# A decoder trunk on one core: identity transposes on TensorE while the program opens, and another order of the last four row tiles

## What is computed

```python
def _rms_norm(x, g):
    y = x * lax.rsqrt(jnp.mean(x * x, axis=-1, keepdims=True) + EPS)
    return y * g

def _short_conv(x, w_in, w_conv, w_out):
    b_gate, c_gate, h = jnp.split(x @ w_in, 3, axis=-1)
    u = causal_depthwise_conv(c_gate * h, w_conv)      # width 3
    return (b_gate * u) @ w_out

for layer in range(2):
    xn = _rms_norm(x, g[0])
    mix = _short_conv(xn, ...) if layer == 0 else _dilated_attention(xn, ...)
    x = x + _rms_norm(mix, g[1])
    ff = _swiglu(_rms_norm(x, g[2]), w_in, w_out)
    x = x + _rms_norm(ff, g[3])
```

## Time and profile before

| | us |
|---|---|
| median of 3 runs | 2272.85 (2272.17 to 2273.74) |
| the profiled execution, its time | 2273.41 |
| the profiled execution, its span from the first to the last instruction | 2271.6 |
| PE busy | 2216.3 (98%) |
| DVE busy | 1687.8 (74%) |
| ACT busy | 962.3 (42%) |
| POOL busy | 485.1 (21%) |
| mean granted clock of PE, share of full speed | 0.997 |

### The profile page before, as it was taken

The page is one execution under the profiler, slowest core; times in us unless marked ns, Lnnn a source line. Parts: engine busy times, 40 slices in busy tenths (PEclk is TensorE's granted clock), DMA queues, the critical chain, the costliest instruction groups (busy, mean ns, idle before and its releaser), DMA issues. The chain is left out here.

```text
span 2271.6 us, 31865 instructions
## 1 busy us (share of the span) xinstructions
PE 2216.3 (98%) x10604; PEld 1848.8 (81%) x10604; DVE 1687.8 (74%) x2529; ACT 962.3 (42%) x1758; POOL 485.1 (21%) x416
## 2 busy tenths in 40 slices
PE   7999998999999999999999999999899999999997
PEld 6888887888888888877888888888788888888886
DVE  6988769777777667797767666676877777776768
ACT  4322345322222243564566566565532222223453
POOL 5000026333333100251110011002533333310113
PEclk9999999999999999999999999999999999999999
DMA  5122242333333477635333233234133333338764
GB/s 158 38 56 56 96 155 61 102 108 98 111 98 112 157 265 241 204 122 161 84 85 84 67 73 83 57 107 144 50 113 107 102 104 105 103 108 281 246 227 171
DMA packets 246010, 278.24 MB, mean 122 GB/s; under 512 B 18528, under 2 KB 157792, under 8 KB 243808
## 3 DMA queue, kind: packets, MB, share of 16 engines
q1 hardware_dynamic: 242656, 264.84, 38.0%
q10 hardware_dynamic: 3200, 11.54, 1.5%
HBM read 202.40 MB, written 48.76 MB: 111 GB/s over the span
## 5 line engine op out<-in xcount | busy, mean ns | idle before, releaser
L1249 PE MATMUL banks<-xb_mid,up_split 128*128 128x512 f32 x2064 | 477.4, 390 | 1.5 <-DVE up_split L2381 1.5
L1249 PEld LDWEIGHTS banks<-xb_mid,up_split 128*128 128x128 f32 x2064 | 388.2, 188 | 82.5 <-DVE up_split L2381 1.9
L1338 PE MATMUL banks<-down_split 128*128 128x512 f32 x1848 | 423.0, 390 | 4.7 <-DVE down_split L2749 3.3
L1338 PEld LDWEIGHTS banks<-down_split 128*128 128x128 f32 x1848 | 345.4, 188 | 80.9 <-DVE down_split L2749 8.1
L1249 PE MATMUL banks<-xb_low,up_split 128*128 128x512 f32 x1584 | 368.8, 391 | 5.6 <-DVE xb_low L2309 2.0
L1249 PEld LDWEIGHTS banks<-xb_low,up_split 128*128 128x128 f32 x1584 | 298.1, 188 | 69.0 <-DVE up_split L2381 4.8
L2749 DVE TENSOR_TENSOR down_split<-down_raw,down_split 128x1024 fp32r<-128x1024 f32 x154 | 198.2, 1287 | 107.3 <-ACT down_split L1955 106.9
L1955 ACT CAST down_split<-down_raw 128x1024 fp32r<-128x1024 f32 x154 | 161.8, 1051 | 204.2 <-PE banks L1338 169.5
L3391 POOL TENSOR_TENSOR sums<-raw_up 128x512 f32<-128x512 f32 x88 | 117.3, 1336 | 482.3 <-DMA raw_up<-in_ffn_in_w 255.1
L1383 PE MATMUL banks<-x_hi,w_second 128*128 128x512 f32 x672 | 176.3, 394 | 0.0
L3062 DVE CUSTOM_DVE_ANT_0 scores<-banks,bias 128x896 f32<-128x896 f32 (+7 forms) x128 | 96.7, 756 | 78.8 <-PE banks L1420 63.5
(11 more groups left out here) (227 smaller groups left out, 3607.8 us busy)
## 6 DMA issues: line engine op xcount, KB each, us to landing
raw_up<-in_ffn_in_w SPq DMA_DIRECT2D x88, 512.0 KB, 5.0
down_raw<-in_ffn_out_w SPq DMA_DIRECT2D x154, 256.0 KB, 3.4
down_raw<-hid_spill SPq DMA_DIRECT2D x154, 256.0 KB, 4.1
hid_spill<-hid_mix SPq DMA_DIRECT2D x110, 256.0 KB, 4.9
down_second<-in_ffn_out_w SPq DMA_DIRECT2D x66, 256.0 KB, 3.3
k_stack<-k_parts SPq DMA_DIRECT2D x32, 512.0 KB, 6.2
hid_spill<-hid SPq DMA_DIRECT2D x44, 256.0 KB, 2.0
raw_up<-in_conv_in_w SPq DMA_DIRECT2D x18, 512.0 KB, 5.2
```

The lines of the kernel that those rows point to most:

```text
L1249: mm = pe.matmul(bank(b_out), up_part(ph, p, a)[:, q * P:(q + 1) * P], block(RIGHT_OF[p], b)[:, q, :], start=(i == 0), stop=(i == len(pass ...
L1338: mm = pe.matmul(bank(b_out), side[:, a, 0, i * P:(i + 1) * P], side[:, b, 1, :], start=(p in (M3, M5, M1, M2) and first and j == 0), stop ...
```

## The change

Three edits, all in the opening. (1) PE issues 78 transposes of the identity matrix into bank 7, whose result nobody reads: 30 before the turn of tile 0, and 16, 10, 16 and 6 behind the turns of tiles 0, 1, 2 and 3. (2) The turns of tiles 4 to 7 stand behind matmuls 1, 11, 23 and 33 of the opening instead of 8, 18, 28 and 38. (3) ACT squares tile 7 directly behind tile 6, ahead of the high part of tile 4.

```diff
-        TURNS_FIRST = {8: HT, 18: HT + 1, 28: HT + 2, 38: HT + 3}
+        TURNS_FIRST = {1: HT, 11: HT + 1, 23: HT + 2, 33: HT + 3}
+        KEPT_BUSY = (30, 16, 10, 16, 6)
...
+            def keep_busy(n):
+
+                for _ in range(n):
+                    pe.transpose(psum[:, 7, 0:P], ident[:], ident[:])
+
             pe.wait_ge(*setup_step.at("norm0", 3))
+            keep_busy(KEPT_BUSY[0])
             for t in range(TT // 2):
                 turn("norm0", t)
+                keep_busy(KEPT_BUSY[t + 1])
...
-                    if i < TT:
+                    if i < TT - 1:
                         second_square("norm0", i)
+                    if i == TT - 2:
+                        second_square("norm0", TT - 1)
                     if i >= lag_split:
                         high_part("norm0", i - lag_split)
```

## The result

The changed kernel is slower: 2276.95 us, median of 19 runs (2275.15 to 2278.9), against 2273.74 for the kernel before, of which 19 runs were now taken too (2271.22 to 2276.25). The ratio is 1.0015, 95% interval 1.0008 to 1.0022. The profiled execution has a span of 2275.1 us, 3.5 more than that of before. The prediction was 2270.5.

The account below looks back on a forecast made before the run. PE, busy 98% of the span, was taken as the bound. Terms 1.65 + 0.29 + 0.41 + 0.39 - 0.09 - 0.36 = 2.29 us off the profiled 2273.41, and 0.56 for the median, gave 2270.5; range 2268.6 to 2274.2.

Parts of the forecast that it names:

- Transposes and the clock: Opening, PE: unbroken identity transposes raise the clock from half to full at 6.8 us; up to 10.7 costs nothing.
- What full clock is worth: Opening: first eight matmuls 1.65 us, turn of tile 4 0.29, ACT's wait 0.41; together 2.35 us saved.
- The fillers are hidden by the loads of x and by ACT, and cost nothing: Opening, ahead of turn 3: 72 of the 78 fillers delay nothing if turn 3 starts by 17.2 us; price nothing.
- What the opening gives up early, the following stage passes on: Behind the opening PE waits for nothing for 230 us, so the opening's gain is handed on.
- Turns of tiles 4 to 7, square of tile 7: Opening: new waits of 0.09 and 0.36 us ahead of turns 4 and 6, 0.39 won at second half; square free.
- fall ahead of the matmuls: Rival, chance 0.25: PE idles after turn 3 and its clock falls again, price 1.55 us, 2272.1; among the turns, 2274.1.
- The rival on which the kernel becomes slower: Ahead of turn 3: identity transposes do not raise the clock, +6.9 us, 2279.7; chance 0.12.
- does not reach the end: Rival, chance 0.08: the 2.3 us won at 34 us are lost later to a load or VectorE, 2272.9.

Follow-up runs that it names:

- e4: The kernel before with 82 filler transposes (30, 16, 10, 16, 10), old places of the turns and old order of the squares; 2281.57 us, ratio 1.0036.
- e5: The changed kernel with 100 semaphore increments that nobody waits for in PE's first feed-forward layer, in front of the loop; 2270.31 us, ratio 0.9985.
- e9: The kernel before with 160 semaphore increments in PE's first feed-forward layer, no fillers, old order; 2285.78 us, ratio 1.0056.
- e10: The changed kernel with 100 semaphore increments in PE's second feed-forward layer, behind the loop; 2276.89 us, ratio 1.0019.
- e8: The changed kernel with 46 fillers (24, 8, 4, 6, 4) instead of 78; 2270.35 us, ratio 0.9985.
- e1: The changed kernel with four more fillers, ten instead of six behind the turn of tile 3; 2283.18 us, ratio 1.0045.

## Why the prediction was wrong

- *Transposes and the clock.* Right. The 30 fillers took 5.88 us, between 30 x 0.108 and 30 x 0.221; with those two prices some 22 ran slowly (an estimate), so the clock went up near 7.7 us (forecast 6.8, needed by 10.7). What full clock is worth was right too: in e4 the first eight matmuls last from 19.31 to 21.24, 1.62 us less than before (forecast 1.65). The rule of the Trainium skill ("TensorE: Matmul & The Clock Gate", Part 4: PE-mode transpose) that full clock does not engage for transposes does not hold here: nothing but transposes ran until 19.43, and the turn at 8.58 took 1.04 us.
- *The fillers are hidden by the loads of x and by ACT, and cost nothing.* This is the step that failed: right for the opening, wrong for the program. I priced a filler by its time on PE alone. Its other price is its room in PE's instruction stream: 156 instructions in front of a loop moved the loop among the packets of q8, and that cost 3.25 and 3.07 us at its two returns, shown by e5, e9 and e10.
- *What the opening gives up early, the following stage passes on.* Right as far as it went: 2.33 us earlier at 38 us, 3.11 ahead of the first stall. My view of the waits ended at 268 us, and a stall on "issue" has no releaser, so nothing in the trace of before pointed at the loop except the missing line of q8 between 1177 and 1420 us, which I did not look for.
- *Turns of tiles 4 to 7, square of tile 7.* Right in sum, wrong in the two waits. The turn of tile 4 starts at 19.88 (forecast 19.70), 0.45 us behind the first matmul; at 0.237 for a matmul that is 0.22 of waiting, where 0.09 was forecast. The turn of tile 5 starts at 23.11 (22.86). The seven matmuls ahead of the turn of tile 6 take 1.67 us (25.14 to 26.81), and 7 x 0.237 is 1.66: at most 0.1 of waiting, where 0.36 was forecast. The start of turn 6 was right all the same (26.81, forecast 26.85), since DVE's norm of tile 6 sets it (it ends at 26.76, forecast 26.81): what PE had lost ahead of turn 4 came off this wait. In all, the new order gives nothing: with it the matmuls that started at 40.30 start 0.03 us later than without it (37.97 against 37.94 in e4), where 0.06 later was forecast.
- *Rivals.* The clock did not fall ahead of the matmuls, in spite of 1.40 us of idling. The rival on which the kernel becomes slower had the wrong mechanism, and "does not reach the end" named loads of data or VectorE and a time of 2272.9, not instructions and a net loss. The range left a loss of this kind out.

That the opening's gain is real is shown by e5 and e8: 3.1 and 3.0 us under the kernel before, taken together with them (2273.39), interval 0.6 to 2.4 thousandths. A difference under the 0.2% of the prediction could therefore be told.

What is shown is that the loop's position decides and that packets are loaded inside it when it stalls; that the reason is one packet too many (A2) is an inference. What stays open: how many packets are held (seven at least, as 1602 instructions cannot lie in fewer), and whether one of them is always the next to be loaded. The shifts 0, 3, 80, 92, 126 and 256 did not stall and 156, 160 and 164 did; the first edge lies between 126 and 156, the second between 164 and 256, and neither was tried closer. If A2 holds, 1602 instructions touch eight packets from 65 of the 256 starting places, so the second edge would lie 65 behind the first, between 191 and 221; this is an estimate that no run tested.

## What to carry to other kernels

Count the instructions that a change puts in front of a loop as well as their time, and compare the packets on the engine's instruction queue inside the loop before and after: if they go from none to some, the returns may stall on "issue" as here, and no semaphore shows for it. If a useful edit stalls a loop, move the loop, by padding to the next whole packet (e5) or by making the edit smaller (e8), before giving up the edit.

## What the runs showed of the hardware

Whether a loop of 1602 PE instructions is loaded again at each return depends on where it begins, and 30 instructions decide: with 126 more in front of it 75 packets were loaded in the whole program, with 156, 93. These are 18 more, nine in each of the two repeated passes (nine from 1174 to 1300.5 us, nine from there to 1426.5): not only the one packet too many, but as many as the whole loop touches and one or two beyond. The Trainium skill ("Runtime: NRT & Kernel Launch", section "Instruction fetch mechanics") says that instructions are refilled in blocks of 16 KiB, 256 instructions, and that a taken branch to a target outside the window held stalls until it is fetched; the packets and the stalls agree with that. The same section of the Trainium skill gives PE room for 2048 instructions, by this eight such blocks, and also speaks of a window of two pages. The two pages do not hold for PE here: a loop of 1602 instructions, at least seven blocks, ran three times without one load. Eight would have room for it, but no run counts what is held.

A return cost 3.1 to 3.3 us in the changed kernel, with 156 instructions. With 160 and 164 (e9, e1, e4) the two stalls of the first return were 1.3 to 1.7 and 2.6 to 3.1 us; behind them the granted clock fell to 0.50, and the matmuls took twice as long for some us. e4 and e1, with eight instructions more than the change, took 4.6 and 6.2 us longer than it, most of that through the clock: PE's waits for "issue" at both returns grew only from 7.0 us to 7.3 and 7.8. The clock can fall with 156 too: in the profiled execution of e10, 2280.08 us and the slowest of its eleven, the granted clock from 1172 to 1190 us was 0.91, where the changed kernel has 1.00.
